# First level of the block inverses in an RWKV-7 stage: VectorE takes chunks 0 and 2, GpSimd keeps 1 and 3

## What is computed

```
def _rwkv7_step(state, inp):
    r, w, k, v, kk, kka = inp
    sa = jnp.einsum('dbhvk,dbhk->dbhv', state, kk)
    state = state * w[..., None, :] - sa[..., :, None] * kka[..., None, :] + v[..., :, None] * k[..., None, :]
    y = jnp.einsum('dbhvk,dbhk->dbhv', state, r)
    return state, y
```

## Time and profile before

| | |
|---|---|
| median of three executions | 1161.42 us |
| the profiled execution | 1163.03 us |
| its span | 1161.2 us |
| TensorE busy | 1143.8 us (98%) |
| VectorE busy | 547.8 us (47%) |
| ScalarE busy | 628.2 us (54%) |
| GpSimd busy | 911.7 us (79%) |
| granted TensorE clock, mean | 0.999 of full |

### The profile page before, as it was taken

The page is one execution under the profiler, slowest core; times in us unless marked ns, Lnnn a source line. Parts: engine busy times, 40 slices in busy tenths (PEclk is TensorE's granted clock), DMA queues, the critical chain, the costliest instruction groups (busy, mean ns, idle before and its releaser), DMA issues.

```text
span 1161.2 us, 24130 instructions
## 1 busy us (share of the span) xinstructions
PE 1143.8 (98%) x10058; PEld 1068.4 (92%) x10058; DVE 547.8 (47%) x987; ACT 628.2 (54%) x1005; POOL 911.7 (79%) x702
## 2 busy tenths in 40 slices
PE   9999999999999999999999999999998999999998
PEld 9998999999998999998999999999888979999997
DVE  5543576543652222224744333657955556333333
ACT  6666666548644644544744444689542327444443
POOL 6988668876986999896999999598652026999994
PEclk9999999999999999999999999999999999999999
DMA  8655445655566565565565665645500024666563
GB/s 284 193 174 170 140 129 164 203 160 156 185 223 203 191 188 185 184 192 183 163 183 185 191 188 183 225 149 174 162 3 3 22 93 164 184 189 190 183 187 102
DMA packets 53628, 192.43 MB, mean 166 GB/s; under 512 B 6288, under 2 KB 7184, under 8 KB 53136
## 3 DMA queue, kind: packets, MB, share of 16 engines
q1 hardware_dynamic: 51792, 184.36, 50.6%
q10 hardware_dynamic: 1728, 6.53, 1.5%
HBM read 188.77 MB, written 1.05 MB: 163 GB/s over the span
## 4 chain that ended last, share of the span: by engine, by line
PE 90%; DVE 5%; ACT 2%; issue 1%; DMA 1%; POOL 0%; SPq 0%; DVEq 0%; ACTq 0%; POOLq 0%
PE product L586 17%; PE product L588 17%; PE product L587 17%; PE bank L698 7%; PE bank L700 7%; PE bank L699 7%; PE bank L1207 3%; PE product L1281 2%; PE product L1207 1%; PE bank L1218 1%; PE product L1167 1%; PE product L797 1%; PE product L799 1%; PE product L798 1%; PE bank L755 1%
## 5 line engine op out<-in xcount | busy, mean ns | idle before, releaser
L536 POOL TENSOR_TENSOR weight_lo<-raw_ring,weight_hi 128x512 fp32r<-128x512 f32 x684 | 890.5, 1335 | 200.7 <-ACT weight_hi L2566 187.3
L2566 ACT ACTIVATE weight_hi<-raw_ring 128x1024 fp32r<-128x1024 f32 x338 | 356.9, 1059 | 365.6 <-DMA raw_ring<-in_ffn_gu 110.2
L586 PE MATMUL product<-operand_B_hi,weight_hi 128*128 128x256 f32 x1104 | 311.9, 283 | 0.2 <-POOL weight_lo L536 0.2
L588 PE MATMUL product<-operand_B_hi,weight_lo 128*128 128x256 f32 x1104 | 311.3, 282 | 0.0
L587 PE MATMUL product<-operand_B_lo,weight_hi 128*128 128x256 f32 x1104 | 310.8, 282 | 0.0
L586 PEld LDWEIGHTS product<-operand_B_hi,weight_hi 128*128 128x128 f32 x1104 | 208.0, 188 | 3.2 <-POOL weight_lo L536 0.4
L587 PEld LDWEIGHTS product<-operand_B_lo,weight_hi 128*128 128x128 f32 x1104 | 207.9, 188 | 3.1
L588 PEld LDWEIGHTS product<-operand_B_hi,weight_lo 128*128 128x128 f32 x1104 | 207.9, 188 | 0.0
L586 PE MATMUL product<-operand_A_hi,weight_hi 128*128 128x256 f32 x712 | 204.5, 287 | 0.1
L588 PE MATMUL product<-operand_A_hi,weight_lo 128*128 128x256 f32 x712 | 200.8, 282 | 0.0
L587 PE MATMUL product<-operand_A_lo,weight_hi 128*128 128x256 f32 x712 | 200.7, 282 | 0.0
(11 more groups left out here) (413 smaller groups left out, 1524.0 us busy)
## 6 DMA issues: line engine op xcount, KB each, us to landing
raw_ring<-in_w_in SPq DMA_DIRECT2D x95, 512.0 KB, 3.5
raw_ring<-in_ffn_gu SPq DMA_DIRECT2D x88, 512.0 KB, 3.5
raw_ring<-in_ffn_down SPq DMA_DIRECT2D x44, 512.0 KB, 3.5
raw_ring<-in_w_mlp_up SPq DMA_DIRECT2D x32, 512.0 KB, 3.5
raw_ring<-in_w_mlp_down SPq DMA_DIRECT2D x32, 512.0 KB, 3.5
raw_ring<-in_w_out SPq DMA_DIRECT2D x16, 512.0 KB, 3.6
raw_ring<-in_w_gmlp_v SPq DMA_DIRECT2D x8, 512.0 KB, 3.5
raw_ring<-in_w_branch_c SPq DMA_DIRECT2D x8, 512.0 KB, 3.5
```

Of the source, the lines that this page charges most:

```text
L536: last = k.nc.gpsimd.tensor_tensor(k.wlo[:, slot, part], k.raw[:, slot, part], k.whi[:, slot, part].bitcast(F32), ALU.subtract)
L586: mm(ps, w_hi, op.hi[:, b, :], start=b == 0, stop=False)
L588: return mm(ps, w_lo, op.hi[:, b, :], start=False, stop=b == blocks - 1)
L2566: k.nc.scalar.activation(k.whi[:, slot, 0:w], k.raw[:, slot, 0:w], ACT.Copy).then_inc(k.s["hi_ready"], 1)
```

## The change

Chunks 0 and 2 get their first inverse on VectorE: two adds, the mask and the transpose in one go, behind the edge products of (0,0) for chunk 0 and of (3,1) for chunk 2. GpSimd keeps chunks 1 and 3. The transposes of chunks 0 and 2 move forward in VectorE's order with it. `st.do` adds 1 to VectorE's own step semaphore and `st.settle()` waits for the last such step. TensorE no longer waits for `tt_first` in the first level.

```diff
@@ -556,24 +556,22 @@
     def first_inverse(j):
 
         if j >= 2:
-            pool.wait_ge(k.s["u_mm"], 10 * (j // 2 - 1) + 9 + j % 2)
+            pool.wait_ge(k.s["u_mm"], 10)
         for d in (1, 0):
             rows = slice(HD * d, HD * d + HD)
             pool.wait_ge(k.s["z_ev"], 4 * j + 4 - 2 * d)
             k.nc.gpsimd.tensor_tensor(k.nt[j % 2][rows], k.z4[j][rows, d, :, :, 0, :].rearrange("p h b t -> p (h b) t"),
                                       k.stack[rows].unsqueeze(1).to_broadcast([HD, 8, RC]), ALU.add).then_inc(k.s["nt_in"], 1)
-            pool.wait_ge(k.s["nt_in"], 2 * j + 2 - d)
+            pool.wait_ge(k.s["nt_in"], 2 * (j // 2) + 2 - d)
         k.nc.gpsimd.tensor_tensor(k.ttc[j], k.nt[j % 2], k.levels[:, 0:1, :].to_broadcast([P, 8, RC]),
                                   ALU.mult).then_inc(k.s["tt_first"], 1)
-        pool.wait_ge(k.s["tt_first"], j + 1)
+        pool.wait_ge(k.s["tt_first"], j // 2 + 1)
 
     pool.wait_ge(k.s["cb_made"], 2)
-    first_inverse(0)
     first_inverse(1)
     ahead = before_rwkv + 5
     low_parts(before_rwkv, ahead)
     pool.wait_ge(k.s["lo_ready"], ahead)
-    first_inverse(2)
     first_inverse(3)
     low_parts(ahead, k.total)
 
@@ -1262,9 +1260,7 @@
     def level_both(j, level):
 
         pe.wait_ge(s["u_ev"], nth(j, level, 5))
-        if level == 1:
-            pe.wait_ge(s["tt_first"], j + 1)
-        else:
+        if level > 1:
             pe.wait_ge(s["tt_ev"], nth(j, level - 1, 5))
         per_unit(LANES[j % 2][0], k.uc[j % 2], k.ttc[j]).then_inc(s["tt_mm"], 1)
 
@@ -2383,9 +2379,23 @@
             nv.tensor_tensor(k.z4[j][:, d, h].rearrange("p b w t -> p b (w t)"), banks[h][:].rearrange("p (b n) -> p b n", b=AB),
                              k.edges[:, d:d + 1, :].to_broadcast([P, AB, P]), ALU.mult).then_inc(s["z_ev"], 1)
 
+    def first_inverse(j):
+
+        if j:
+            v.wait_ge(s["u_mm"], 9)
+        v.wait_ge(s["z_ev"], 4 * j + 4)
+        for d in (1, 0):
+            rows = slice(HD * d, HD * d + HD)
+            st.do(nv.tensor_tensor(k.nt[j % 2][rows], k.z4[j][rows, d, :, :, 0, :].rearrange("p h b t -> p (h b) t"),
+                                   k.stack[rows].unsqueeze(1).to_broadcast([HD, 8, RC]), ALU.add))
+        st.settle()
+        st.do(nv.tensor_tensor(k.ttc[j], k.nt[j % 2], k.levels[:, 0:1, :].to_broadcast([P, 8, RC]), ALU.mult))
+        st.settle()
+
     def first_turned(j):
 
-        v.wait_ge(s["tt_first"], j + 1)
+        if j % 2:
+            v.wait_ge(s["tt_first"], j // 2 + 1)
         nv.transpose(flat(k.tc[j % 2]), flat(k.ttc[j])).then_inc(s["t_ev"], 1)
 
     def nth(j, level, levels):
@@ -2485,10 +2495,11 @@
     v.wait_ge(s["masks_in"], 32)
     chunk_products(0, 1, LANES[0])
     chunk_products(0, 0, LANES[1])
+    first_inverse(0)
+    first_turned(0)
     chunk_products(1, 1, SPARE_BANKS)
     chunk_products(1, 0, LANES[0])
     attention_out(0)
-    first_turned(0)
     attention_scores(2)
     level_left(0, 1)
     attention(6)
@@ -2507,9 +2518,10 @@
     chunk_products(2, 0, LANES[0])
     attention(16)
     chunk_products(3, 1, LANES[1])
+    first_inverse(2)
+    first_turned(2)
     attention(18)
     chunk_products(3, 0, SPARE_BANKS)
-    first_turned(2)
     first_turned(3)
     for level in range(1, 6):
         level_left(2, level)
```

## The result

| | before | changed |
|---|---|---|
| median | 1162.13 us (4 executions) | 1169.22 us (4 executions) |
| the profiled execution | 1163.03 us | 1169.65 us |
| its span | 1161.2 us | 1167.8 us |
| VectorE busy | 547.8 us | 549.4 us |
| GpSimd busy | 911.7 us | 904.1 us |

The ratio is 1.0059, 95% interval 1.0047 to 1.0071, or +6.9 us (5.5 to 8.3) on 1162. Forecast were +4.86 us and 1166.3 (on a median of 1161.42, from the first three of the four executions), in a range up to 1168.6. The direction was right; the time lies above the range.

What follows compares the result with a forecast made beforehand. The prediction took TensorE to bound the kernel, with VectorE's queue delaying it at two places. First pair 2.27 plus second pair 2.59 made 4.86 us, on a median of 1161.42 giving 1166.3 us, range 1164.2 to 1168.6.

Steps and rivals of the forecast that it cites:

- Where the time is decided: RWKV stage, chunk pairs 0/1 and 2/3: delays to TensorE's next instruction move the end; nothing behind gives them back.
- Price of the four instructions on VectorE: Two adds, mask and transpose behind the fourth edge product: fourth to fifth product 3.40 us against 0.60, 2.80 more.
- First pair, 2.27: Chunks 0 and 1: VectorE's queue delays keys_by_token(1) and turned_probabilities(1), so scores(1) starts late; costs 2.27 us.
- The waits of 1.8 and some 0.7: TensorE, first pair: waits of 1.8 us for edge products on line 2383, then some 0.7 for attention_out(0).
- Second pair, 2.59: Chunks 2 and 3: four VectorE instructions plus turns with GpSimd's add make attention_out(7) and the last product 2.59 us late.
- The meeting: Second pair: VectorE's adds and GpSimd's first add of chunk 3 take turns; cost 2.59 us with it, 1.44 without.
- The queue: Second pair without turns: four instructions delay attention_out(7), the 1.34 us gap hides part, 1.44 us is left.
- The Trainium skill's rule of the shared port: VectorE instructions with two SBUF inputs and GpSimd instructions reading SBUF alternate whole; applied to second pair, 2.59 instead of 1.44.
- rival B: TensorE's granted clock falls behind a 4.1 us stop at the second pair; 2 us in all, 1168.3; chance 0.09.
- A: Second pair: VectorE's and GpSimd's adds do not meet or block; 2.27 + 1.44 = 3.7 us, 1165.1; chance 0.17.
- C: First pair nearly free, adds at half price on 64 partitions; +1.6 us, 1163.0; chance 0.08.
- D: Faster: GpSimd's queue keeps chunk 3 late, so removing chunk 2 ends waits of 3.2 us; 1158.2; chance 0.02.

Runs made afterwards that it cites:

- e1: Kernel before with only chunk 0's first inverse moved to VectorE, chunk 2 left on GpSimd; 1.0030 against the kernel before, +3.5 us.
- e3b: Changed kernel plus unneeded TensorE identity products fitted to its waits (6, 2, 16 and 5); 1164.22 us against 1168.96 for the changed kernel.
- e4: Changed kernel, but GpSimd's first add of chunk 3 also waits for VectorE's transpose of chunk 2; 1.0051 against the kernel before.
- e8: Changed kernel's split, with VectorE's inverses later in its list, behind the work TensorE waits for; 1170.91 us, 1.0072 against the kernel before.
- e6: Kernel before with one VectorE order changed: products of (3,0) ahead of attention_out(7); 1160.74 us, 0.9979 against the kernel before.
- e7b: Kernel before with (3,0) products ahead of attention_out(7) and VectorE taking all of chunk 3's first inverse but one add; 1159.81 us against 1162.05, 0.9969.
- e2: Kernel before with only chunk 2's first inverse moved to VectorE, chunk 0 left on GpSimd; 1.0024 against the kernel before, +2.8 us.
- e3: Changed kernel plus unneeded TensorE identity products in its stops (10, 4, 28 and 9), which overran the waits; 1167.48 us against 1161.99 before, 1.0049.
- e5: Changed kernel with fitted TensorE filler (6, 2, 11, 5) and GpSimd's first add of chunk 3 held until VectorE's transpose of chunk 2; 1.0005 against before.
- e10: Kernel before with 5 and 6 filler products in TensorE's two waits at the second place, nothing else; 1160.96 us, 0.9982 against the kernel before.

## Why the prediction was wrong, step by step

- **Where the time is decided.** Right: the two places of the earlier trace rows, and nothing given back behind them. d is 0.84 shorter and the start 0.38 later in the one pair of profiles; d differs by 0.90 between the two profiles of the changed kernel itself.
- **Price of the four instructions on VectorE.** Right: 3.51 for 3.40 from fourth to fifth product; on 64 partitions an add took 0.70, the mask on 128 took 0.69.
- **First pair, 2.27.** By the queue 2.43 (e1, e3b). The waits of 1.8 and some 0.7 that I had drawn up were 1.77 and 0.66. But 1.41 by the clock comes on top, and no part of the forecast had it.
- **Second pair, 2.59.** b grew by 2.60, and so close a match is luck, since two errors cancel. The meeting is 0.95, for 1.15. The queue is 1.65 (b of e4 less that of before), for 1.44: I had started the add 0.60 behind the product here and 0.72 behind it at the first place, and the wait for the product's own end takes 0.71 at both (886.22 to 886.93). c was to stay; without the clock it shrinks by 0.30 (e3b), with it it grows by 0.62.
- **The Trainium skill's rule of the shared port** (SBUF — State Buffer, "Who interferes with whom"). The trace agrees: 2.36 for 1.40 in the changed kernel, 1.40 when the two are kept apart (e4), and in e8 3.32 for the adds beside GpSimd's add and mask and 1.64 for VectorE's mask beside a low part.
- **The failed step is the size and chance of rival B.** I gave the clock's fall 0.09 and only to the second place, with the argument that the stop there is longer than any of before, and the sum had it at nothing. It fell at both places in both profiles of the changed kernel, and a clock under 1.00 was one of the prediction's own signs of being wrong. At the first, stops of 1.77 and 0.66 with 1.1 of work between them saw it fall in the changed kernel and not in e1; in e1 it fell behind the old stop of 1.58. What it costs is 0.92 us at the second place, where I had put 2, and 1.41 at the first, where I had put nothing. That my 2 is near the total of 2.33 is luck. This term belonged into the sum: 4.86 + 2.33 = 7.2, or 1168.6 on the median forecast from, against +6.9 measured. The Trainium skill (TensorE: Matmul & The Clock Gate, "Why this matters for your kernels") warned of such gaps; the trace agrees at the second place, and shows a fall at the first behind shorter ones.
- **Rivals A, C and D.** A needed adds of 0.7 each; they took 2.36 together. C needed adds at half price; they took 0.70 each where nothing met them. D needed GpSimd's queue as the cause; e6 and e7b show that it is the last product's end and the chain behind it. e7b gains 2.24 of the 3.2 that D looked for, by taking most of chunk 3 off GpSimd and not chunk 2.

## What to carry to other kernels

An engine that is half idle can still be the wrong place for more work: price what stands behind the new instructions in its queue, and give it the work that lies behind the last event on the chain, not the work that can run ahead. Where VectorE and GpSimd both read two operands from SBUF, count their instructions in turn, even when they are off the chain. And where a change lets TensorE stand for a microsecond or more in several pieces, add the clock's fall to the sum for each such place, at the work that follows it, or fill the stop. At the first place the fall came in three profiles of the four with the delays of the change; it came at each of the six stops of 3.2 us or more, in the two profiles of the changed kernel, e2, e4 and twice in e8.

## What the runs showed of the hardware that was not expected

The clock's fall is not settled by the lengths of the stops: those of 1.77 and 0.66 saw it fall in the changed kernel and not in e1, one of 1.58 saw it fall in e1 and not in the profile of before. One and the same kernel differs too: executions of before have mean clocks from 0.995 to 1.000. What decides between them was not tried. At the lower level 32 products of 64x64 took 1.97 us instead of 1.15 to the end of the last, and in the profiles the clock stayed down for about 3 to 7 us.

TensorE also stops in the middle of a run of 64x64 products for no reason that the profile shows ("issue"). In the kernel before, at 931 and 943 us:

```profile
931.06 0.62 PE L1207 MATMUL product<-arena 64*64 64x64 f32 x14 [1.14 <-issue]
...
943.24 1.03 PE L1207 MATMUL product<-arena 64*64 64x64 f32 x28 [1.47 <-issue]
```

In e3b the same 32 products of each group run through:

```profile
933.07 1.10 PE L1205 MATMUL product<-arena 64*64 64x64 f32 x32
...
943.98 1.10 PE L1205 MATMUL product<-arena 64*64 64x64 f32 x32
```

Stops of this kind, of 0.7 to 1.5 us, are in every profile of a kernel without filler, once or twice, and in none of e3, e3b and e5, with 24 to 51 filler products; e10, with 11, has one. They differ between two executions of one kernel: the two profiles of the changed kernel have 0.86 and 1.39, and one of 1.10. The filler kernels are thus up to 2.6 us faster in d than before for a reason that is not the clock. That it has to do with where in TensorE's list these products lie is argued and not shown, and what makes the stops was not tried. Of the 3.9 us by which e3b's d is shorter than that of before, they are 2.6, and the rest stays open.
